# A two-block sequence model on one core: where the latent attention's keys are made

## The chip, the cores and the metric

The kernel runs on one core of a Trainium2 chip. Its time is the device time of one execution in microseconds (us); the median of three runs before the change is 2564.14 us (2563.71 to 2564.52). One more execution was profiled; it took 2568.02 us.

The engines are named as the profile names them: PE is the matrix engine (PEld its weight loads), ACT, DVE and POOL are the scalar, vector and GpSimd engines, SP issues most of the DMAs. Each engine works through its own instructions in order and waits at semaphores.

## The reference

Two transformer-like blocks over 512 tokens of width 1024, all in float32. The first block has three parts: a gated delta rule, a multi-head latent attention, and a feed-forward part. Only the attention matters here; cut to that:

```python
ckv = rms_norm(c_kv, kv_norm_w)                              # 512 x 256
k_nope = (ckv @ w_uk).reshape(B, S, 8, 128)                  # a key per head
v = (ckv @ w_uv).reshape(B, S, 8, 128)
k = concatenate([k_nope, broadcast(k_rope, 8 heads)], -1)    # 128 + 64
q = rms_norm(q, q_norm_w); k = rms_norm(k, k_norm_w)         # over all 192
... the last 64 of q and k are rotated by position
sc = einsum('bqhd,bkhd->bhqk', q[:, s0:s1], k[:, :s1]) * 192 ** -0.5
p = softmax(where(chunk mask, sc, -inf))                     # blocks of 128 queries
out = einsum('bhqk,bkhd->bqhd', p, v)
```

So for each head the key needs a projection (`w_uk`), the sum of squares of its 192 entries for each token, the inverse root of that, and a product with it.

## The kernel before, in words

One program is written out five times, once for each engine and once as a plan of the weights (`Plan`, `Tensor` for PE, `Scalar` for ACT, `Vector` for DVE, `Gpsimd` for POOL). Each stage is a generator; `program` (L813) runs them, and a `yield` is a step. `weave(main, side, n, m)` takes m steps of `side` over n steps of `main`. All engines take the same steps, so the order on every engine is fixed when the kernel is built.

Large linear layers work on one unit of weights at a time, 128x8x128 or 512 KB. SP loads it into one of three slots of `wraw`; ACT copies it to `whi` (rounded), then DVE (odd units) or POOL (even units) subtracts to get `wlo`; PE then does 24 passes of 512 columns for a unit (8 blocks of the input, each three times: `hhi,whi`, `hlo,whi`, `hhi,wlo`). I call these 24 passes a **layer step**. The call `ahead(i)` puts the splitting of all units up to number i+2 at that place of ACT's, DVE's and POOL's order. The units of `w_uk` (128 KB, one for each head) aren't split: PE multiplies straight from `wraw`, and their slot is free only when PE has done so. They are units of the same list and take slots of the same three.

While the attention runs, its steps are woven with the side work `beside`: the projections z0, z1, gd, gm and ya (layer steps), `o_norms` (the norms of the delta rule's output, matmuls with a matrix of ones), `z_gate` (eight Silu on ACT), `gates` (eight Sigmoid) and `split_o`. The main part is `norms_then`: `mla_norms` (values, last query norms, the five rotations) and then `mla_heads`, in which two heads go side by side, four pairs in all.

One head (`mla_head`) takes these steps:

- the key's projection on PE into a PSUM bank (`uk`); ACT squares it into `SCR[e]`; DVE adds the part of the rotary key (`SCR[e]+KQ`)
- a matmul with ones sums over partitions (`un`); ACT takes Ln and Exp of it, the inverse root; DVE multiplies the bank by it into `KN[e]` and the rotary key into `KZ[e]`; only then the bank of `uk` is free
- for the four blocks of queries: scores on PE (`mla_scores`), maximum on DVE, Exp on ACT, scaling on DVE, transposes on PE (`ps<-cst,...`), a copy on ACT, the product with the values on PE.

There is one `KN` and one `KZ` for even heads and one for odd ones, so the key of head h+2 can be written only after head h's last scores. Five PSUM banks (ps3 to ps7) serve all of the attention and the norms; ps0 to ps2 serve the layer steps. `KZ[e]` has 128 rows of which 64 hold zeros (set by POOL with one MEMSET behind the recurrence), so that it meets only its half of `QR`.

Of the kernel before, what the change touches and what calls it, by code (L numbers as in the profile page):

```python
# [7 lines left out]
P = 128  # L8
# [277 lines left out]
def build(nc, D, out, known):  # L286
# [5 lines left out]
    with ctx:  # L292
# [163 lines left out]
        KZ = [A[:, 18 + j, :] for j in range(2)]  # L456
# [5 lines left out]
        GM = [A[:, i, :] for i in (38, 39, 40, 41, 29, 23, 21, 22)]  # L462
# [115 lines left out]
        ADA_SUM = [SCR[3], SCR[4]]  # L578

# [72 lines left out]
        class Stages:  # L652
# [157 lines left out]
            prep = recur = early_norms = mla_norms = mla_head = o_norms = z_gate = gates = split_o = ple = conv = idle  # L810
            sv_norms = spatial = att_pairs = gla = idle

        def program(f):  # L813
# [17 lines left out]
            weave(f.norms_then(), side, 56, 38)  # L831
# [51 lines left out]
        class Plan(Stages):  # L883
# [51 lines left out]
            def mla_head(self, h):  # L935
                W.add(("uk", h), False, 2, P, [(rows(D["mla_w_uk"][0], 0, 2, h * P, P), 0)], ("ma_mm", "uk", h))
                for _ in range(11):
                    yield


        class Tensor(Stages):
# [372 lines left out]

            def mla_head(self, h):
                e = h % 2
                v = self.raw(("uk", h))
                bk = PA.take("uk", h)
                pe.wait_ge(*PA.free("uk", h))
                for k in range(2):  # L1320
                    pe.wait_ge(*at("mq_ve", "ck", k))
                    t = mm(bk[:, :], v[:, k, :], CKV[k], k == 0, k == 1)
                t.then_inc(*inc("ma_mm", "uk", h))
                yield
                bk = PA.take("un", h)
                pe.wait_ge(*PA.free("un", h))
                pe.wait_ge(*at("ma_ve", "sq", h))
                mm(bk[:, :], ones, SCR[e], True, True).then_inc(*inc("ma_mm", "un", h))
                PA.put(("un", h), "ma_act", "ln", h)
                PA.put(("uk", h), "ma_ve", "kn", h)  # L1330
                yield
# [26 lines left out]
            def mla_scores(self, h, i):  # L1358
                e = h % 2
# [6 lines left out]
                mm(bk[:, 0:Lk], ON[h][:, s], KN[e][:, 0:Lk], True, False)  # L1366
                pe.wait_ge(*at("ma_ve", "kz", h))
                pe.wait_ge(*at("ro_po", "r", h // 2))
                mm(bk[:, 0:Lk], QR[h // 2][:, s], KZ[e][:, 0:Lk], False, False)
# [213 lines left out]
        class Scalar(Stages):  # L1583
# [224 lines left out]

            def mla_head(self, h):
                e = h % 2  # L1810
                self.ahead(W.index["uk", h])
                ac.wait_ge(*at("ma_mm", "uk", h))
                ac.wait_ge(*(at("ma_ve", "kz", h - 2) if h >= 2 else at("mq_ve", "ck", 1)))
                act(SCR[e], PA.of("uk", h)[:, :], ACT.Square).then_inc(*inc("ma_act", "sq", h))
                yield
                ac.wait_ge(*at("ma_mm", "un", h))
                act(SCR[e], PA.of("un", h)[:, :], ACT.Ln, bias=kcol(K_EPS), scale=1.0 / 192).then_inc(*inc("ma_act", "ln", h))
                ac.wait_ge(*at("ma_act", "ln", h))
                act(SCR[e], SCR[e], ACT.Exp, scale=-0.5).then_inc(*inc("ma_act", "ri", h))
                yield  # L1820
# [446 lines left out]
        class Vector(Stages):  # L2267
# [291 lines left out]

            def mla_head(self, h):  # L2560
                e = h % 2
                rs = slice(64 * e, 64 * e + 64)
                self.ahead(W.index["uk", h])
                ve.wait_ge(*at("ma_act", "sq", h))
                ve.wait_ge(*at("mq_ve", "kq"))
                tt(ve, SCR[e], SCR[e], KQ, ALU.add).then_inc(*inc("ma_ve", "sq", h))
                yield
                ve.wait_ge(*at("ma_act", "ri", h))
                if h >= 2:
                    ve.wait_ge(*at("ma_mm", "s", h - 2, 3))  # L2570
                stt(KN[e], PA.of("uk", h)[:, :], col("kn"), SCR[e], ALU.mult, ALU.mult).then_inc(*inc("ma_ve", "kn", h))
                ve.wait_ge(*at("ro_po", "z"))
                tt(ve, KZ[e][rs], KR[rs], SCR[e][rs], ALU.mult).then_inc(*inc("ma_ve", "kz", h))
                yield
# [49 lines left out]
            def ev_gm(self, m, bk):  # L2624
                ve.wait_ge(*at(*lin_done("gm", m)))
                ve.wait_ge(*at("ro_po", "r", 3))
                cp(ve, GM[m], bk[:, :]).then_inc(*inc("mix_ve", "gm", m))

# [322 lines left out]
        class Gpsimd(Stages):  # L2951
# [92 lines left out]
            def mla_norms(self):  # L3044
# [4 lines left out]
                for p in SG.ends("rec"):  # L3049
                    po.wait_ge(*p)  # L3050
                ms(po, A[:, 18:20, :], 0.0).then_inc(*inc("ro_po", "z"))
# [6 lines left out]
            def mla_head(self, h):  # L3058
                self.ahead(W.index["uk", h])
                for _ in range(11):  # L3060
                    yield
# [252 lines left out]
```

## Time and profile before

| | us |
|---|---|
| median of three runs | 2564.14 |
| the profiled execution | 2568.02 |
| its span, first to last instruction | 2566.2 |
| PE busy in the span | 2361.6 |
| norms, attention and side work (628 to 951 us of the span) | 323 |
| PE busy in these 323 us | 276.1 |
| granted TensorE clock, whole span | 0.954 |

The page gives busy time per engine, and the chain of work that ended last: PE has 74% of it. The attention's stage lies from about 628 us (the rotations start) to 951 us (the output projection starts). Pairs of heads start at about 671, 713, 788 and 863 us. Times in rows are us from the start of the span. In rows of the time line the columns are start, length, engine, line, operation, and in brackets the idle time of that engine just before, with what ended it. `ps<-scr,cst` of 128x512 is the sum over partitions (`un`), `ps<-arena,wraw` the projection (`uk`), `ps<-nab` ends a block of scores.

### The profile page before, as it was taken

Reading aid. Unit: us, or ns where it says so; the run is one execution under the profiler, and the core shown is the slowest. Engines: PE = TensorE matmul, PEld = TensorE weight load, DVE = VectorE, ACT = ScalarE, POOL = GpSimd, SP = SyncE. Lnnn points to the kernel's source line nnn. Section 1 sums busy time; section 2 is a strip of 40 time slices with the busy share of each in tenths; the row PEclk is TensorE's granted clock in tenths of the full one; section 3 lists DMA queues with packets and bytes.
Section 4 is the critical chain, followed back from the end, with each engine's and each line's share of the span. In section 5 each row is a group of like instructions: output and inputs, shape, how many; then the busy total and the mean of one; then the engine's idle time right before and its main releaser. Section 6 shows DMA issues by size and latency. Waiting matters only on the chain.

```text
span 2566.2 us, 27004 instructions
## 1 busy us (share of the span) xinstructions
PE 2361.6 (92%) x10928; PEld 1894.9 (74%) x10928; DVE 1085.4 (42%) x1580; ACT 924.4 (36%) x1350; POOL 701.7 (27%) x416
## 2 busy tenths in 40 slices
PE   8798989999798899899999888999999999999996
PEld 4577877985566677688888676787777777888875
DVE  2576655454433332433321499513444243322333
ACT  2544423223432432533322332334552433322334
POOL 1141144002011125322223232321232353432332
PEclk9898989999899899899999898999999999999998
DMA  8222223121122124333333422232211322333341
GB/s 261 74 66 70 70 58 99 50 82 33 37 62 68 43 82 119 103 102 95 95 96 96 123 82 66 82 92 82 82 58 58 114 83 82 107 91 99 99 123 50
DMA packets 347983, 220.66 MB, mean 86 GB/s; under 512 B 18393, under 2 KB 327244, under 8 KB 347860
## 3 DMA queue, kind: packets, MB, share of 16 engines
q1 hardware_dynamic: 338462, 202.31, 27.3%
q10 hardware_dynamic: 9398, 16.62, 1.9%
q8 instruction: 88, 1.44, 0.2%
q14 instruction: 35, 0.29, 0.0%
HBM read 210.49 MB, written 8.41 MB: 85 GB/s over the span
## 4 chain that ended last, share of the span: by engine, by line
PE 74%; DVE 11%; ACT 8%; POOL 2%; issue 2%; DMA 2%; ACTq 0%; SPq 0%; DVEq 0%; POOLq 0%
PE ps L342 73%; DVE arena L368 4%; ACT arena L357 3%; DVE arena L360 2%; ACT scr L357 1%; DVE scr L368 1%; PE ps L345 1%; ACT whi L357 1%; POOL arena L360 1%; DMA wraw<-in_w_in_dram 1%; POOL wlo L360 1%; ACT L353 1%; DVE scr L360 1%; DVE wlo L360 1%; DVE arena L365 1%
## 5 line engine op out<-in xcount | busy, mean ns | idle before, releaser
L360 POOL TENSOR_TENSOR wlo<-wraw,whi 128x1024 fp32r<-128x1024 f32 (+1 forms) x163 | 390.8, 2398 | 1229.4 <-ACT whi L357 1229.4
L342 PE MATMUL ps<-hhi,whi 128*128 128x512 f32 x1664 | 678.3, 408 | 50.6 <-POOL wlo L360 31.2
L342 PE MATMUL ps<-hlo,whi 128*128 128x512 f32 x1664 | 661.9, 398 | 0.0
L342 PE MATMUL ps<-hhi,wlo 128*128 128x512 f32 x1664 | 661.2, 397 | 0.0
L357 ACT ACTIVATE whi<-wraw 128x1024 fp32r<-128x1024 f32 (+1 forms) x328 | 340.7, 1040 | 347.8 <-PE ps L342 294.7
L342 PEld LDWEIGHTS ps<-hhi,whi 128*128 128x128 f32 x1664 | 322.1, 194 | 131.6 <-issue 44.5
L342 PE MATMUL ps<-arena 128*128 128x128 f32 (+4 forms) x2304 | 337.1, 302 | 40.0 <-ACT arena L357 17.5
L342 PEld LDWEIGHTS ps<-hlo,whi 128*128 128x128 f32 x1664 | 322.0, 194 | 68.5 <-issue 3.7
L342 PEld LDWEIGHTS ps<-hhi,wlo 128*128 128x128 f32 x1664 | 320.8, 193 | 70.0
L360 DVE TENSOR_TENSOR wlo<-wraw,whi 128x1024 fp32r<-128x1024 f32 (+2 forms) x165 | 213.3, 1292 | 372.6 <-ACT whi L357 372.4
L342 PEld LDWEIGHTS ps<-arena 128*128 128x128 f32 x2304 | 291.4, 198 | 70.0 <-ACT arena L357 22.0
L357 ACT ACTIVATE arena<-ps 128x512 f32<-128x512 f32 (+5 forms) x223 | 116.6, 541 | 333.5 <-PE ps L342 269.0
L342 PE MATMUL ps<-h,whi 128*128 128x512 f32 x512 | 159.9, 394 | 1.1 <-POOL wlo L360 1.1
L357 ACT ACTIVATE scr<-ps,colv 128x512 f32<-128x512 f32 x78 | 55.5, 713 | 243.9 <-PE ps L342 243.7
L368 DVE SCALAR_TENSOR_TENSOR scr<-ps,colv,scr 128x511 f32<-128x511 f32 (+2 forms) x116 | 86.7, 748 | 132.9 <-ACT scr L357 130.5
L368 DVE SCALAR_TENSOR_TENSOR arena<-arena,colv 128x512 f32<-128x512 f32 (+1 forms) x136 | 131.7, 973 | 12.2 <-ACT arena L357 8.6
L360 DVE TENSOR_TENSOR arena<-ps,arena 128x512 f32<-128x512 f32 (+1 forms) x88 | 55.6, 639 | 147.4 <-PE ps L342 145.2
L360 DVE TENSOR_TENSOR scr<-ps,scr 128x512 f32<-128x512 f32 x86 | 59.1, 689 | 138.9 <-PE ps L342 137.2
L342 PEld LDWEIGHTS ps<-h,whi 128*128 128x128 f32 x512 | 97.2, 190 | 22.8 <-issue 2.6
L360 POOL TENSOR_TENSOR arena<-arena,scr 128x512 f32<-128x512 f32 x57 | 76.9, 1353 | 135.1 <-ACT scr L357 96.5
L342 PE MATMUL ps<-ff,whi 128*128 128x512 f32 x352 | 108.2, 389 | 0.0
L371 DVE COPY arena<-ps 128x512 f32<-128x512 f32 (+3 forms) x60 | 38.4, 652 | 150.3 <-PE ps L342 138.5
(190 smaller groups left out, 2729.1 us busy)
## 6 DMA issues: line engine op xcount, KB each, us to landing
wraw<-in_w_in_dram SPq DMA_DIRECT2D x99, 512.0 KB, 3.9
wraw<-in_w_ff_dram SPq DMA_DIRECT2D x64, 512.0 KB, 4.0
wraw<-in_ffn_w_up_dram SPq DMA_DIRECT2D x44, 512.0 KB, 3.8
wraw<-in_w_ada_dram SPq DMA_DIRECT2D x32, 512.0 KB, 3.9
wraw<-in_w_gate_dram SPq DMA_DIRECT2D x32, 512.0 KB, 3.9
arena<-in_w_ada_dram SPq DMA_DIRECT2D x8, 1024.0 KB, 11.5
wraw<-in_ffn_w_down_dram SPq DMA_DIRECT2D x16, 512.0 KB, 4.1
wraw<-in_w_branch_dram SPq DMA_DIRECT2D x16, 512.0 KB, 3.5
```

The source lines that it names most:

```text
L342: return pe.e.matmul(o, l, r, start=start, stop=stop)
L345: return pe.e.transpose(o, i, CST[0:n, C_ID:C_ID + n])
L353: ac.e.preload_act_table_set("natural_log_exp_and_others")
L357: return ac.e.activation(o, i, f, bias=bias, scale=scale, **kw)
L360: return q.e.tensor_tensor(o, a, b, op)
L365: return q.e.tensor_scalar(o, a, s1, s2, op0, op1)
L368: return ve.e.scalar_tensor_tensor(out=o, in0=a, scalar=s, in1=b, op0=op0, op1=op1)
L371: return q.e.tensor_copy(o, i)
```

## The change

`mla_head` loses its first two steps. They become `mla_keys(g)`, which makes the keys of both heads of a pair in three steps. `mla_heads` takes these steps for the next pair beside the present one (behind the steps 1, 3 and 5 of the pair, counted from 0), `norms_then` those of the first pair beside the norms. With it:

- the keys get tiles of their own: `KNB(h)` is in blocks 16/17, 40/41, 16/17, 54/55 of the arena for the four pairs, `KZB(h)` takes 64 rows of block 18 or 19, half each for the two heads; the rotary scores use 64 rows of both operands, and POOL's MEMSET goes
- the bank of `uk` is read earlier: DVE first writes `KNB = bank * col("kn")` (`kr`), which frees the bank, and later multiplies `KNB` by the inverse root in place, one DVE instruction more for each head
- new waits: `KNB` of heads 4 and 5 waits for the last scores of 0 and 1, that of head 6 for the projection of head 7 (blocks 54 and 55 hold the latent), `GM` gets another order of blocks, and its last two wait for scores of heads 2 and 3
- a head now has 9 steps in place of 11; the weave is 47 to 38 in place of 56 to 38.

```diff
+        def KNB(h):
+            return A[:, (16, 40, 16, 54)[h // 2] + h % 2, :]
+        def KZB(h):
+            return A[64 * (h % 2):64 * (h % 2) + 64, 18 + h // 2 % 2, :]
...
             def mla_heads(self):
                 for h in range(0, 8, 2):
-                    yield from both(self.mla_head(h), self.mla_head(h + 1))
+                    keys = self.mla_keys(h + 2) if h < 6 else iter(())
+                    for n, _ in enumerate(both(self.mla_head(h), self.mla_head(h + 1))):
+                        if n in (1, 3, 5):
+                            next(keys, None)
+                        yield
 
             def norms_then(self):
-                yield from self.mla_norms()
+                keys = self.mla_keys(0)
+                for n, _ in enumerate(self.mla_norms()):
+                    if n in (4, 5, 6):
+                        next(keys, None)
+                    yield
...
-            weave(f.norms_then(), side, 56, 38)
+            weave(f.norms_then(), side, 47, 38)
...
+            def mla_keys(self, g):                       # Vector
+                for h in (g, g + 1):
+                    self.ahead(W.index["uk", h])
+                    ve.wait_ge(*at("ma_act", "sq", h))
...
+                    ts(ve, KNB(h), PA.of("uk", h)[:, :], col("kn"), None, ALU.mult).then_inc(*inc("ma_ve", "kr", h))
+                    ve.wait_ge(*at("mq_ve", "kq"))
+                    tt(ve, SCR[h % 2], SCR[h % 2], KQ, ALU.add).then_inc(*inc("ma_ve", "sq", h))
+                yield
+                yield
+                for h in (g, g + 1):
+                    rs = slice(64 * (h % 2), 64 * (h % 2) + 64)
+                    ve.wait_ge(*at("ma_act", "ri", h))
+                    ve.wait_ge(*at("ma_ve", "kr", h))
+                    tt(ve, KNB(h), KNB(h), SCR[h % 2], ALU.mult).then_inc(*inc("ma_ve", "kn", h))
...
+                    tt(ve, KZB(h), KR[rs], SCR[h % 2][rs], ALU.mult).then_inc(*inc("ma_ve", "kz", h))
```

How instructions move, at three places. First PE at the end of the first pair of heads, before the change. `ps7<-arena` and `ps4<-arena` are the products with the values, `arena,wraw` the two projections, `scr,cst` the two sums.

```order
L342 MATMUL ps7<-arena 128x128 x3
L342 MATMUL ps4<-arena 128x128 [waits s_ma_act]
L342 MATMUL ps4<-arena 128x128 x3
L342 MATMUL ps4<-arena,wraw 128x512 [waits s_ob,s_raw1]
L342 MATMUL ps4<-arena,wraw 128x512
L342 MATMUL ps5<-arena,wraw 128x512 [waits s_raw2]
L342 MATMUL ps5<-arena,wraw 128x512
L342 MATMUL ps6<-scr,cst 128x512 [waits s_ma_ve]
L342 MATMUL ps7<-scr,cst 128x512 [waits s_ma_ve]
L342 MATMUL ps2<-hhi,whi 128x512 [waits s_w_lo_ve,s_w_hi,s_mix_ve]
```

The same place after the change: the products with the values, then a layer step (24 passes, cut here), then the scores of the next pair.

```order
L342 MATMUL ps7<-arena 128x128 x3
L342 MATMUL ps4<-arena 128x128 [waits s_ma_act]
L342 MATMUL ps4<-arena 128x128 x3
L342 MATMUL ps2<-hhi,whi 128x512 [waits s_w_lo_ve,s_w_hi,s_mix_ve]
...
L342 MATMUL ps7<-arena 128x128 [waits s_ob]
L342 MATMUL ps7<-arena 128x128 [waits s_ro_po]
L342 MATMUL ps7<-nab 128x128
```

The four instructions of the projections and the two sums are gone from this place. The projections now stand here, in the middle of the pair before, right behind its second block of scores and right ahead of a layer step:

```order
L342 MATMUL ps3<-arena 128x256 [waits s_ma_act]
L342 MATMUL ps3<-arena 128x256
L342 MATMUL ps3<-nab 128x128
L342 MATMUL ps5<-arena,wraw 128x512 [waits s_ma_act,s_raw0]
L342 MATMUL ps5<-arena,wraw 128x512
L342 MATMUL ps6<-arena,wraw 128x512 [waits s_ma_act,s_raw2]
L342 MATMUL ps6<-arena,wraw 128x512
L342 MATMUL ps2<-hhi,whi 128x512 [waits s_w_lo_po,s_w_hi,s_mix_ve]
```

The last row is the start of the layer step; it waits for both halves of its weights, the second of which POOL makes.

ACT at the same place, before: the Exps of the first two blocks of both heads with the splits of two units around them (`whi<-wraw`).

```order
L357 ACTIVATE whi<-wraw 128x1024 [waits s_mm,s_raw2]
L357 ACTIVATE arena,small<-ps3,small 128x128 [waits s_ma_ve]
L357 ACTIVATE scr,small<-ps5,small 128x128 [waits s_ma_ve]
L357 ACTIVATE arena,small<-ps6,small 128x256 [waits s_ma_ve]
L357 ACTIVATE scr,small<-ps3,small 128x256 [waits s_ma_ve]
L357 ACTIVATE whi<-wraw 128x1024 [waits s_mm,s_raw0]
L357 ACTIVATE arena<-ps5 128x128 [waits s_ma_mm]
```

And after: no split is left ahead of the four Exps, and three stand behind them, around the two squares of the next pair's keys (`scr<-ps5`, `scr<-ps6`).

```order
L357 ACTIVATE arena,small<-ps3,small 128x128 [waits s_ma_ve]
L357 ACTIVATE scr,small<-ps5,small 128x128 [waits s_ma_ve]
L357 ACTIVATE arena,small<-ps6,small 128x256 [waits s_ma_ve]
L357 ACTIVATE scr,small<-ps3,small 128x256 [waits s_ma_ve]
L357 ACTIVATE whi<-wraw 128x1024 [waits s_mm,s_raw1]
L357 ACTIVATE scr<-ps5 128x512 [waits s_ma_mm]
L357 ACTIVATE whi<-wraw 128x1024 [waits s_mm,s_raw0]
L357 ACTIVATE scr<-ps6 128x512 [waits s_ma_mm]
L357 ACTIVATE whi<-wraw 128x1024 [waits s_mm,s_raw1]
L357 ACTIVATE arena<-ps3 128x128 [waits s_ma_mm]
```

The first of the three splits belongs to the layer step that PE reaches right behind the projections: it used to be made a layer step earlier.

ACT also gets two table loads more, 67 in place of 65 in the whole program: four Silus now stand between the Exps of the first pair's third and last blocks (they stood behind the last), with a load on either side.

## Rows read from the trace of the kernel before

**Rows 1.** The page: busy time, clock in 40 slices, us to a DMA's landing.
```profile
PE 2361.6 (92%) x10928; PEld 1894.9 (74%) x10928; DVE 1085.4 (42%) x1580; ACT 924.4 (36%) x1350; POOL 701.7 (27%) x416
...
PEclk9898989999899899899999898999999999999998
...
wraw<-in_w_in_dram SPq DMA_DIRECT2D x99, 512.0 KB, 3.9
```

**Rows 2.** Stretches: width, busy of five engines, granted clock, DMA share, GB/s.
```profile
628.00:665.00 37.00, 23.51 (x45) 9.80 (x43) 16.75 (x19) 17.68 (x28) 14.42 (x10) 0.75 0.17 46
665.00:713.00 48.00, 42.29 (x197) 34.27 (x195) 16.94 (x43) 16.08 (x37) 2.39 (x1) 0.91 0.05 15
713.00:799.00 86.00, 74.36 (x317) 55.10 (x317) 33.01 (x59) 28.20 (x51) 11.87 (x5) 0.95 0.26 65
...
875.00:951.00 76.00, 66.85 (x293) 52.41 (x292) 27.36 (x51) 33.31 (x59) 16.16 (x9) 0.89 0.23 67
```

**Rows 3.** PE's waits from 628 to 952 us: total, times, longest.
```profile
PE ps L342 <- DVE scr L360: 16.3, 4, 5.7
PE ps L342 <- ACT arena L357: 11.7, 8, 5.0
PE ps L342 <- DVE arena L368: 10.7, 3, 7.1
PE ps L345 <- ACT arena L357: 3.6, 2, 3.3
```

**Rows 4.** Time line where the third pair starts.
```profile
787.86 3.59 PE L342 MATMUL ps<-arena,wraw 128*128 128x512 f32 x8
...
790.40 0.69 DVE L360 TENSOR_TENSOR scr<-scr,arena 128x512 f32<-128x512 f32 x1 [0.53 <-ACT scr L357]
...
793.70 1.06 ACT L357 ACTIVATE whi<-wraw 128x1024 fp32r<-128x1024 f32 x1 [3.33 <-DMA wraw<-in_w_in_dram]
...
794.84 2.35 POOL L360 TENSOR_TENSOR wlo<-wraw,whi 128x1024 fp32r<-128x1024 f32 x1 [24.18 <-ACT whi L357]
...
795.28 2.46 DVE L360 TENSOR_TENSOR scr<-scr,arena 128x512 f32<-128x512 f32 x1 [4.18 <-ACT scr L357]
...
797.79 2.07 PE L342 MATMUL ps<-scr,cst 128*128 128x512 f32 x2 [5.47 <-DVE scr L360]
...
803.43 0.39 PE L342 MATMUL ps<-hhi,whi 128*128 128x512 f32 x1
```

**Rows 5.** Time line where the norms end and the first pair starts.
```profile
657.46 2.08 PE L342 MATMUL ps<-scr,cst 128*128 128x512 f32 x2 [7.14 <-DVE arena L368]
...
661.76 3.78 PE L342 MATMUL ps<-arena,cst 128*128 128x512 f32 x4 [2.22 <-DVE arena L368]
...
664.56 1.42 PE L342 MATMUL ps<-hhi,whi 128*128 128x512 f32 x1
```

**Rows 6.** Time line of the second pair, behind its second block of scores.
```profile
734.69 0.41 PE L342 MATMUL ps<-nab 128*128 128x128 f32 x1
...
736.26 1.05 ACT L357 ACTIVATE whi<-wraw 128x1024 fp32r<-128x1024 f32 x1
...
737.38 2.39 POOL L360 TENSOR_TENSOR wlo<-wraw,whi 128x1024 fp32r<-128x1024 f32 x1 [14.98 <-ACT whi L357]
```

**Rows 7.** Time line around the Silus (first pair) and the Sigmoids (fourth pair).
```profile
701.24 1.28 ACT L357 ACT_TABLE_LOAD   x1
...
702.53 2.19 ACT L357 ACTIVATE arena<-arena 128x512 f32<-128x512 f32 x4
...
705.14 1.65 PE L342 MATMUL ps<-arena 128*128 128x128 f32 x6 [5.00 <-ACT arena L357]
...
887.98 0.48 PE L345 MATMUL ps<-cst,scr 128*128 128x128 f32 x1 [3.33 <-ACT arena L357]
```

**Rows 8.** PE's groups by shape, 500 to 960 us: busy, mean ns.
```profile
L342 PE MATMUL ps<-scr,cst 128*128 128x512 f32 x28 | 18.9, 764 | 23.4 <-DVE scr L360 16.3 <-DVE arena L368 7.1
...
L342 PE MATMUL ps<-scr,cst 64*128 64x512 f32 x12 | 6.7, 641 | 0.0
```

More of the change, by code:

```diff
@@ L461, in build @@
         MIX = [A[:, 30 + i, :] for i in range(8)]
[L462 removed]
+        GM = [A[:, i, :] for i in (38, 39, 29, 23, 21, 22, 40, 41)]
         XR = [A[:, 42 + i, :] for i in range(8)]
@@ L933, in build @@
             early_norms = steps(8)
[L935 to L938, printed above, removed]
+            def mla_keys(self, g):
+                for h in (g, g + 1):
+                    W.add(("uk", h), False, 2, P, [(rows(D["mla_w_uk"][0], 0, 2, h * P, P), 0)], ("ma_mm", "uk", h))
+                yield
+                yield
+                yield
+            mla_head = steps(9)
         class Tensor(Stages):
@@ L1313, in mla_norms, with mla_keys @@
                 yield
-            def mla_head(self, h):
[L1316 to L1331, printed above, removed]
+            def mla_keys(self, g):
+                for h in (g, g + 1):
+                    v = self.raw(("uk", h))
+                    bk = PA.take("uk", h)
+                    pe.wait_ge(*PA.free("uk", h))
+                    for k in range(2):
+                        pe.wait_ge(*at("mq_ve", "ck", k))
+                        t = mm(bk[:, :], v[:, k, :], CKV[k], k == 0, k == 1)
+                    t.then_inc(*inc("ma_mm", "uk", h))
+                    PA.put(("uk", h), "ma_ve", "kr", h)
+                yield
+                for h in (g, g + 1):
+                    bk = PA.take("un", h)
+                    pe.wait_ge(*PA.free("un", h))
+                    pe.wait_ge(*at("ma_ve", "sq", h))
+                    mm(bk[:, :], ones, SCR[h % 2], True, True).then_inc(*inc("ma_mm", "un", h))
+                    PA.put(("un", h), "ma_act", "ln", h)
+                yield
+                yield
+            def mla_head(self, h):
                 obk = PA.take("mo", h)
@@ L1365, in mla_scores @@
                 pe.wait_ge(*at("mq_ve", "qn", h))
-                mm(bk[:, 0:Lk], ON[h][:, s], KN[e][:, 0:Lk], True, False)
+                mm(bk[:, 0:Lk], ON[h][:, s], KNB(h)[:, 0:Lk], True, False)
                 pe.wait_ge(*at("ma_ve", "kz", h))
                 pe.wait_ge(*at("ro_po", "r", h // 2))
-                mm(bk[:, 0:Lk], QR[h // 2][:, s], KZ[e][:, 0:Lk], False, False)
+                mm(bk[:, 0:Lk], QR[h // 2][rs, s], KZB(h)[:, 0:Lk], False, False)
                 pe.wait_ge(*at("st_po", "nab"))
@@ L1807, in mla_norms, with mla_keys @@
                     yield
-            def mla_head(self, h):
[L1810 to L1820, printed above, removed]
+            def mla_keys(self, g):
+                for h in (g, g + 1):
+                    e = h % 2
+                    self.ahead(W.index["uk", h])
+                    ac.wait_ge(*at("ma_mm", "uk", h))
+                    ac.wait_ge(*(at("ma_ve", "kz", h - 2) if h >= 2 else at("mq_ve", "ck", 1)))
+                    act(SCR[e], PA.of("uk", h)[:, :], ACT.Square).then_inc(*inc("ma_act", "sq", h))
+                yield
+                for h in (g, g + 1):
+                    e = h % 2
+                    ac.wait_ge(*at("ma_mm", "un", h))
+                    act(SCR[e], PA.of("un", h)[:, :], ACT.Ln, bias=kcol(K_EPS), scale=1.0 / 192).then_inc(*inc("ma_act", "ln", h))
+                    ac.wait_ge(*at("ma_act", "ln", h))
+                    act(SCR[e], SCR[e], ACT.Exp, scale=-0.5).then_inc(*inc("ma_act", "ri", h))
+                yield
+                yield
+            def mla_head(self, h):
                 self.mla_exp(h, 0)
@@ L3056, in mla_norms, with mla_keys @@
                 yield
[L3058 to L3061, printed above, removed]
+            def mla_keys(self, g):
+                for h in (g, g + 1):
+                    self.ahead(W.index["uk", h])
+                yield
+                yield
+                yield
+            mla_head = Plan.mla_head
             o_norms, z_gate, gates = Plan.o_norms, Plan.z_gate, Plan.gates
```

42 lines of the change are left out of this document (22 added, 20 removed).

## The prediction

> **What bounds the kernel now.** I read the page first: PE is busy 92% of the span, the other engines 42% or less, and the clock's row falls below full speed at many places [rows 1]. So time is lost where PE idles or runs at 1.2 GHz. Next the table by stretches shows where this change works: between 628 and 951 us PE is busy 276 of 323 us, and the granted clock is lowest in the stretches where pairs start and norms end, 0.75 and 0.89 [rows 2]. The list of PE's waits then says for what. 16.3 us in four waits are for DVE's `scr` (the sum `SCR+KQ` of the keys), 10.7 us in three for DVE's `arena L368` (the key written from its bank), 11.7 and 3.6 us for ACT [rows 3].
>
> The time line shows the first kind [rows 4]. PE makes both projections (3.59 us). ACT's second square stands behind a split that waits 3.33 us for a DMA, because two of three weight slots were held by `w_uk`; then DVE's sum takes 2.46 us, and PE has nothing queued in between that is allowed to run: idle 5.47 us. When it restarts at 797.79, a pass of 512 columns takes twice as long until 803.43 (0.39 us in the row there; the start-to-start distance falls from 0.43 to 0.23 us): 1.2 GHz after the idle time, 2.4 GHz from then on. These 5.6 us at half speed cost 2.8 us more.
>
> The second kind is at the norms' end [rows 5]: `un` of head 1 waits 7.14 us for a DVE instruction, not for its data but for the bank that head 0's projection holds until its key is written, and the next norm waits 2.22 us for head 1's in the same way. The remaining 1.3 us of the 10.7 are in the last pair.
>
> **The change part by part.** The profiled execution took 2568.02 us, and the terms are taken from it; the median of the runs shown is 3.9 us lower.
>
> *Key chains at three pair starts.* The projections and sums leave the place where PE has nothing else, and get two layer steps and a block of scores between them. Their own work (8 passes in 3.59 us, so 0.45 each [rows 4], and 4 passes, 1.8 us) stays on PE. What goes is the idle time: 16.3 + 1.3 = 17.6 us [rows 3]. What is late next there: the scores of the next pair wait for the bank of `mo`, which ACT frees beside the layer step that now stands in between, so I take 0.
>
> *The clock behind them.* Three times 2.8 us [rows 4] = 8.4 us. In the last pair more runs slow: the clock of 0.89 over 76 us [rows 2] is 8.4 us of full speed lost, some of it while PE idled and some behind the Sigmoids, which stay. I give the key chain about half of it, 4.4 us, which is 1.6 more than the 2.8 counted. Bounds: 0, if the clock falls for other small gaps, and 12.
>
> *Norms and first pair.* The bank stalls go, 7.14 + 2.22 = 9.4 us [rows 5]: the bank is now free after the square and one DVE instruction. What is left is the chain of the output norms: four groups of two, each with two squares, the sums, Ln and Exp twice and two DVE products. ACT alone needs six activations for a group, some 3.5 us (four in 2.19 us [rows 7], a little more from PSUM), and DVE's rotations wait for POOL between them (POOL is busy 14.4 us here [rows 2]). 19 PE matmuls of two passes, 0.9 us, have to pass in the same order. Adding up group by group from 629 us, I get the first layer step at 653 with everything at its short duration, and 658 with DVE's and POOL's longer ones and some of it at 1.2 GHz, against 664.56 [rows 5]. I take 6.5 us; bounds 2 and 10. POOL's MEMSET lies in idle time of POOL: 0.
>
> *A weight split that comes later.* `ahead` counts `w_uk` as units, so the layer step behind the projections gets its `whi` only after the four Exps. By the times of the second pair [rows 6]: scores end at 735.10, ACT is done with the last Exp and starts the split at 736.26, `whi` ends at 737.31, POOL's `wlo` at 739.77, 4.7 us after the scores. PE has the projections to do, 3.6 us. New wait 1.1 us, in the first and second pair; in the third DVE makes `wlo` in half the time and two transposes lie in between, so 0. -2.2 us. The next split waits for a slot that the projection frees; 3.9 us for the DMA [rows 1] and 1.06 for `whi` end about 7 us behind the scores, and PE needs what ACT has queued behind it (copies of transposes) at 9.4 us at the earliest, in the third pair. So it hides, with some 2 us to spare. If that cover goes, each us counts.
>
> *Silus and Sigmoids.* Four Silus after the first pair's last Exp cost PE 5.00 us [rows 7]. After the change they stand ahead of the last two Exps, with a load on both sides: 1.28 + 2.19 + 1.28 = 4.75 us of ACT, during which PE has both last blocks of scores and two products (an estimate of 4.5 us, 22 passes of up to 512 columns). By my count PE then waits 0.35, 1.15 and 0.85 us, 2.35 in all: +2.6 us. At the Sigmoids of the last pair PE now arrives with full speed and waits 4.7 where it waited 0.94 + 3.33 [rows 7]: -0.4. The 0.78 us wait for ACT ahead of the second pair's projections goes: +0.8.
>
> By the Trainium skill ("ScalarE: Activation LUTs", What ACT_TABLE_LOAD costs) each switch costs 2.66 us, load and drain. The trace does not agree: the next activation starts 1.29 us after the load's start [rows 7]. By the page the two extra loads would cost ACT 5.3 instead of 2.6 us, and the sum would be up to 2.8 us smaller.
>
> *More DVE work.* Eight more products of two SBUF tiles. Bounds 0.69 and 2.46 us each [rows 4], 5.5 to 20 us of an engine that is busy for a third of this stage; the nearest rows beside an idle POOL say 0.69. On PE's path only in the norms, where it is in the 658 above. The second rotary matmul has 64 rows instead of 128: shapes of 64 rows took 641 ns, full ones 764 at both clocks mixed [rows 8], so 0. The second sum (`un`) waits for the Exp of the block just scored, about as long as the other head's block takes; I take -1.0 for what is over, bounds 0 and -3.
>
> Sum: 17.6 + 8.4 + 1.6 + 6.5 - 2.2 + 2.6 - 0.4 + 0.8 - 1.0 = 33.9 us. 2568.0 - 33.9 = 2534.1 for a profiled execution, 2564.1 - 33.9 = 2530 for the median.
>
> **The rivals.**
>
> *ACT stuck behind weights.* ACT's order now has three splits in a row behind the Exps, each waiting for a slot and a DMA. If the landing is late, ACT's copies are late and PE stalls in the middle of each pair instead of at its end. For it: 3.33 us of exactly this wait in [rows 4], and only 2 us of cover. Against it: PE has two layer steps of 5.5 us (24 passes of 0.23) there in two of three pairs. Price: 3.9 us (one landing) three times and the 8.4 us of the clock: 20 us, so 2550.
>
> *DVE and POOL in each other's way in the norms.* The keys' new products fall among POOL's ten rotation instructions. The same sum took 0.69 us with POOL idle and 2.46 with POOL's `wlo` beside it [rows 4]. If each of the eight DVE instructions of keys and norms there is stretched by up to 1.8 us, the stage gains nothing: 2530 + 6.5, and the clock stays low in it, 3 more: 2540. The Trainium skill ("SBUF — State Buffer", SBUF: two separate sides) says that a DVE instruction with two SBUF inputs and a GpSimd instruction exclude each other for the whole instruction. By that rule the trace agrees in the 2.46, which is POOL's end at 797.19 and a usual 0.69 less overlap.
>
> *Slower than before.* The four products that end the keys (two of `KNB`, two of `KZB`) stand on DVE between the Exps of the last scores and their scaling, for which PE's transposes wait. If all four take 2.46 us, and the scaling stands behind them, that is 9.8 us in each of three pairs, and 2.8 us of clock behind each: 38 us, against the 34 gained, so 2568. It decides from about 11 us per pair. Against it: POOL works only 11.9 us in 86 there [rows 2], so most of these instructions meet an idle POOL.
>
> *It does nothing.* PE's waits move to other places of equal length because weights bound the stage. Against it: the DMA share is at most 0.26 in the stage [rows 2]. 2564.
>
> **How the numbers follow.** Forecast 0.70 (2530), ACT behind weights 0.12 (2550), DVE and POOL 0.10 (2540), slower 0.05 (2568), nothing 0.03 (2564). The forecast's own bounds: all good ends (norms 10, clock 12, no waits) give 34 + 3.5 + 2 + 3 = 42, 2522; the bad ends (norms 2, waits twice, half of the clock) 34 - 4.5 - 3 - 5 = 21, 2543. With ACT's case the range goes to 2552, and I set its low end at 2518 for gaps whose clock cost I count nowhere. A measurement of this kernel can't tell less than 0.2% (5.1 us) from no change: faster 0.92, same 0.03, slower 0.05.
>
> **What the profile after will show.** PE's waits for DVE `scr` and `arena L368` in the stage fall from 27 to under 5 us; a new wait of about 1 us for POOL `wlo` behind the projections in two pairs; the first layer step after the norms starts 4 to 8 us earlier behind the last one of the norms; the wait at the Silus is split and about half; the one at the Sigmoids stays above 4 us; the clock of the pair starts is near 1.0, that of the last pair still below. The stage shrinks from 323 to about 289 us, everything behind it keeps its length. I'm wrong if PE waits for ACT `arena` grow by more than 5 us, or if the gap goes and the clock stays.

## The result and the profile after

The changed kernel takes 2551.06 us (median of 4 runs, 2550.77 to 2552.32) against 2564.2 us of the kernel before (4 runs beside it, 2563.71 to 2564.52), a ratio of 0.9947 with a 95% interval of 0.9935 to 0.9959. It is faster by 13.1 us where 33.9 were forecast: inside the range of 2518 to 2552, but at its slow end. Its profiled execution has a span of 2548.8 us, against 2566.2.

The stage by stretches, each from a pair start to the next one (columns as in [rows 2]):

```profile
628.00:664.00 36.00, 26.56 (x62) 12.41 (x61) 20.76 (x23) 18.71 (x30) 14.25 (x10) 0.86 0.08 22
664.00:720.00 56.00, 49.45 (x210) 34.38 (x209) 25.71 (x54) 24.61 (x47) 4.74 (x2) 0.94 0.16 43
720.00:791.00 71.00, 69.44 (x309) 50.87 (x307) 25.71 (x53) 22.74 (x42) 12.44 (x5) 1.00 0.27 71
791.00:855.00 64.00, 62.94 (x280) 45.80 (x280) 24.66 (x51) 23.76 (x45) 10.10 (x4) 1.00 0.27 75
855.00:932.00 77.00, 70.25 (x294) 51.54 (x293) 26.66 (x50) 28.78 (x53) 16.27 (x9) 0.91 0.21 61
628.00:932.00 304.00, 278.64 (x1147) 195.00 (x1146) 123.50 (x230) 118.59 (x217) 57.80 (x30) 0.95 0.21 58
```

And the stage of before as one row:

```profile
628.00:951.00 323.00, 276.10 (x1152) 204.52 (x1151) 118.78 (x222) 115.77 (x213) 54.37 (x29) 0.90 0.20 55
```

PE's idle time falls from 323.0 - 276.1 = 46.9 us to 304.0 - 278.6 = 25.4. The clock rises from 0.90 to 0.95, with two pairs at 1.00. Both came as forecast. But PE's *busy* time, which should shrink when the clock rises, grew by 2.5 us. PE is doing something longer.

PE's waits in the stage of after (628 to 945 us; total, times, longest):

```profile
PE ps L342 <- ACT arena L357: 10.7, 9, 4.9
PE ps L345 <- DVE arena L364: 4.6, 2, 3.8
PE ps L345 <- ACT arena L357: 4.0, 1, 4.0
PE ps L342 <- POOL wlo L360: 2.5, 2, 1.3
PE ps L342 <- DVE scr L360: 1.0, 1, 1.0
```

Against [rows 3] the 16.3 us for DVE's `scr` are 1.0 and the 10.7 us for DVE's key are gone. What PE does longer is seen in its own time line where the first pair starts. Before:

```profile
671.50 0.60 PE L342 MATMUL ps<-arena 128*128 128x128 f32 x4
671.86 0.30 PE L342 MATMUL ps<-nab 128*128 128x128 f32 x1
672.00 0.66 PE L342 MATMUL ps<-arena 128*128 128x128 f32 x4
...
672.56 1.08 PE L342 MATMUL ps<-arena 128*128 128x256 f32 x4
```

After:

```profile
664.10 0.80 PE L342 MATMUL ps<-arena 128*128 128x128 f32 x4
664.82 0.33 PE L342 MATMUL ps<-nab 128*128 128x128 f32 x1
664.99 0.85 PE L342 MATMUL ps<-arena 128*128 128x128 f32 x4
665.77 0.33 PE L342 MATMUL ps<-nab 128*128 128x128 f32 x1
665.93 1.27 PE L342 MATMUL ps<-arena 128*128 128x256 f32 x4
```

The first score block (four passes for nope and rotary, one for the mask) took 672.00 - 671.50 = 0.50 us and now takes 664.99 - 664.10 = 0.89. Nobody is waited for and the clock is full. The two blocks of 128 columns together: 1.06 before, 1.83 after. The weight loads' rows (660 to 930 us; busy and mean ns, then idle time before them) say where in the block it lies. After:

```profile
L342 PEld LDWEIGHTS ps<-arena 64*128 64x128 f32 x64 | 9.8, 192 | 15.1 <-issue 14.1
L342 PEld LDWEIGHTS ps<-nab 128*128 128x128 f32 x32 | 6.2, 192 | 15.1 <-issue 14.1
```

Before, the mask's row:

```profile
L342 PEld LDWEIGHTS ps<-nab 128*128 128x128 f32 x32 | 6.8, 213 | 3.5 <-issue 2.2
```

In after, 14.1 us of unexplained idle time ("issue") stand ahead of the 64-row loads and 14.1 ahead of the mask's 128-row loads that follow them. They are not the loss itself, since a load runs beside a matmul where nothing holds it, but they sit at exactly the two places of each block where the number of rows changes.

### The profile page after: what moved, and what is told of

Same layout as the page of the kernel before. It is cut to its first block, busy times and chain, and to the rows that moved or that the text cites. A ratio compares the mean times of both kernels' runs of the same rounds, so it can differ in the third digit from the quotient of the medians.

```text
span 2548.8 us, 27018 instructions
## 1 busy us (share of the span) xinstructions
PE 2361.8 (93%) x10928; PEld 1883.4 (74%) x10928; DVE 1090.6 (43%) x1588; ACT 926.9 (36%) x1352; POOL 699.7 (27%) x415
## 3 DMA queue, kind: packets, MB, share of 16 engines
q1 hardware_dynamic: 338462, 202.31, 27.3%
## 4 chain that ended last, share of the span: by engine, by line
PE 76%; DVE 11%; ACT 7%; issue 3%; POOL 2%; DMA 1%; ACTq 0%; SPq 0%; DVEq 0%; POOLq 0%
PE ps L342 74%; DVE arena L368 4%; ACT arena L357 3%; DVE arena L360 2%; DVE scr L368 1%; PE ps L345 1%; POOL wlo L360 1%; ACT whi L357 1%; ACT scr L357 1%; ACT L353 1%; POOL arena L360 1%; DVE wlo L360 1%; DVE arena L365 1%; DVE scr L360 0%; POOL scr L360 0%
## 5 line engine op out<-in xcount | busy, mean ns | idle before, releaser
L342 PEld LDWEIGHTS ps<-hhi,whi 128*128 128x128 f32 x1664 | 322.0, 194 | 134.7 <-issue 47.6
L342 PE MATMUL ps<-arena 128*128 128x128 f32 (+6 forms) x2304 | 341.6, 301 | 34.7 <-ACT arena L357 12.9
L342 PEld LDWEIGHTS ps<-arena 128*128 128x128 f32 (+1 forms) x2304 | 286.7, 197 | 70.0 <-issue 28.3
L368 DVE SCALAR_TENSOR_TENSOR arena<-arena,colv 128x512 f32<-128x512 f32 (+1 forms) x136 | 132.0, 975 | 16.3 <-ACT arena L357 12.6
L360 POOL TENSOR_TENSOR arena<-arena,cst 128x512 f32<-128x512 f32 (+1 forms) x48 | 62.2, 1309 | 144.3 <-PE ps L342 76.7
```

Source lines behind the costliest of these rows:

```text
L342: return pe.e.matmul(o, l, r, start=start, stop=stop)
L360: return q.e.tensor_tensor(o, a, b, op)
L368: return ve.e.scalar_tensor_tensor(out=o, in0=a, scalar=s, in1=b, op0=op0, op1=op1)
```

## The experiments

Theory T1: each change between 128 rows and 64 rows on PE costs time, twice in each of 32 score blocks. Rival T2: the shortfall went into waits and clock, and the longer blocks cover time in which PE would have waited anyway.

The medians carry some 3 us of noise. The programs are the same up to the stage, yet a mark in the norms (the restart behind the 1 us wait for `scr`) stands at 634.1 to 640.9 us in the executions profiled. So the length of the stage from that mark to the output projection is given beside the median: 931.87 - 634.96 = 296.9 us for the changed kernel. It comes from one execution each, and the same stage of the kernel before came out 3.0 us apart in two executions (below), so a difference of some 3 us in it is not told from noise either.

**The rotary matmul with all rows again** (the changed kernel otherwise):

```
-            return A[64 * (h % 2):64 * (h % 2) + 64, 18 + h // 2 % 2, :]
+            return A[:, 18 + h % 2, :]
-                mm(bk[:, 0:Lk], QR[h // 2][rs, s], KZB(h)[:, 0:Lk], False, False)
+                mm(bk[:, 0:Lk], QR[h // 2][:, s], KZB(h)[:, 0:Lk], False, False)
...
-                    if h >= 4:
-                        ve.wait_ge(*at("ma_mm", "s", h - 4, 3))
-                    tt(ve, KZB(h), KR[rs], SCR[h % 2][rs], ALU.mult).then_inc(*inc("ma_ve", "kz", h))
+                    ve.wait_ge(*at("ro_po", "z"))
+                    if h >= 2:
+                        ve.wait_ge(*at("ma_mm", "s", h - 2, 3))
+                    tt(ve, KZB(h)[rs], KR[rs], SCR[h % 2][rs], ALU.mult).then_inc(*inc("ma_ve", "kz", h))
...
+                ms(po, A[:, 18:20, :], 0.0).then_inc(*inc("ro_po", "z"))
```

> The changed kernel with one part of the change undone: the rotary score matmul gets all 128 rows again (KZ in two zero-padded tiles, one per head, written once the head before the last has been scored; one MEMSET on POOL more). Theory T1, the switch of the array from 128 rows to 64 and back costs about 0.4 us in each of 32 score blocks (0.50 became 0.89 us in the first block of 128 columns, 2.22 became 2.72 us in the one of 512): 12.9 us come back, 2551.1 becomes 2538, and PE's weight loads for the mask lose their idle time before them (15.1 us falls to about 3.5). Rival T2, the missing 20 us went into new waits for DVE, POOL and ACT and into the clock, and the longer blocks only show where PE would have waited anyway: within 2 us of 2551, PE's idle time in the stage grows by what the blocks lose.

Measured: 2535.95 us (2533.81 to 2537.67), ratio 0.9886, 0.9872 to 0.9901. 15.1 us came back; stage 917.36 - 634.61 = 282.8 us, 14.2 less. Its first pair and its mask loads:

```profile
663.71 0.60 PE L342 MATMUL ps<-arena 128*128 128x128 f32 x4
664.07 0.30 PE L342 MATMUL ps<-nab 128*128 128x128 f32 x1
664.22 0.66 PE L342 MATMUL ps<-arena 128*128 128x128 f32 x4
...
664.77 1.08 PE L342 MATMUL ps<-arena 128*128 128x256 f32 x4
```

```profile
L342 PEld LDWEIGHTS ps<-nab 128*128 128x128 f32 x32 | 6.2, 195 | 3.3 <-issue 2.2
```

The block takes 0.51 us again. The weight loads show what the change of rows does. In after, the first block of 256 columns (PEld):

```profile
665.87 0.30 PEld L342 LDWEIGHTS ps<-arena 128*128 128x128 f32 x2
666.51 0.29 PEld L342 LDWEIGHTS ps<-arena 64*128 64x128 f32 x2 [0.33 <-issue]
```

The same block with full rows:

```profile
664.71 0.73 PEld L342 LDWEIGHTS ps<-arena 128*128 128x128 f32 x4
```

With full rows the four loads follow each other, beside the matmuls. In after, the first 64-row load starts at 666.51, together with its own matmul, and not beside the pass ahead of it. The rows above merge instructions; the single records of the 512-column blocks give the price of one change. Passes of equal rows start 0.43 us apart, the first 64-row pass 0.52 behind the last 128-row one (698.38 - 697.86), and the second 64-row pass 0.53 behind the first: 0.09 + 0.10 = 0.2 us. The way back to 128 rows costs 0.2 us in the same way.

T2 is out: PE's idle time in the stage is 289.0 - 261.7 = 27.3 us, 1.9 more than in the changed kernel, while the busy time is 16.9 less.

```profile
628.00:917.00 289.00, 261.73 (x1145) 195.22 (x1143) 122.06 (x230) 118.13 (x216) 57.51 (x29) 0.96 0.22 61
```

**The kernel before with 64 rows, and nothing else:**

```
+                rs = slice(64 * e, 64 * e + 64)
-                mm(bk[:, 0:Lk], QR[h // 2][:, s], KZ[e][:, 0:Lk], False, False)
+                mm(bk[:, 0:Lk], QR[h // 2][rs, s], KZ[e][rs, 0:Lk], False, False)
```

> The kernel before with this one part of the change alone: the second score matmul reads only the 64 rows of its head (QR and KZ sliced), nothing else. T1: 32 blocks x 0.4 us, 2564.1 becomes about 2577. T2: no change, within 2 us of 2564; my prediction's step said 0 as well.

Measured: 2577.66 us (2576.87 to 2579.79), ratio 1.0048, 1.0032 to 1.0065: 13.3 us slower. The same two loads (660 to 950 us; busy and mean ns, then idle time):

```profile
L342 PEld LDWEIGHTS ps<-arena 64*128 64x128 f32 x64 | 10.6, 208 | 15.9 <-issue 15.0 <-DVE arena L360 0.2
L342 PEld LDWEIGHTS ps<-nab 128*128 128x128 f32 x32 | 6.6, 205 | 16.0 <-issue 15.2
```

So it is this part of the change alone, in both surroundings.

**The two 64-row matmuls side by side** (the changed kernel, other order in a block):

```
...
+                if h % 2:
+                    mm(bk[:, 0:Lk], QR[h // 2][rs, s], KZB(h)[:, 0:Lk], True, False)
+                    mm(bk[:, 0:Lk], ON[h][:, s], KNB(h)[:, 0:Lk], False, False)
+                    mm(bk[:, s], NAB[:, 0:P], NAB[:, P:2 * P], False, True)
+                else:
+                    mm(bk[:, 0:Lk], ON[h][:, s], KNB(h)[:, 0:Lk], True, False)
+                    mm(bk[:, s], NAB[:, 0:P], NAB[:, P:2 * P], False, False)
+                    mm(bk[:, 0:Lk], QR[h // 2][rs, s], KZB(h)[:, 0:Lk], False, True)
...
```

> The changed kernel (64-row rotary matmul) with another order of the three matmuls of a score block: the even head takes nope, mask, rotary, the odd head rotary, nope, mask, so that the two 64-row matmuls of a pair stand side by side and the array goes from 128 rows to 64 and back 16 times instead of 32. If the cost belongs to each switch from 128 rows to 64 and back (0.4 us), half of it returns: 2551 becomes about 2544.5, and PE's weight loads for the mask that stand behind a 128-row matmul lose their idle time. If it belongs to each 64-row matmul by itself, wherever it stands, 2551 stays. If the pair of 64-row matmuls even runs side by side in the array, it is below 2543.

Measured: 2545.14 us (2543.67 to 2546.83), ratio 0.9920, 0.9905 to 0.9935; stage 928.32 - 636.33 = 292.0 us, 4.9 less. The expected number came out, but my count of half the switches was wrong: in the blocks of 384 and 512 columns the product of the probabilities stands between the two heads' blocks, so only the first two sizes are joined, 8 places. There it is worth more than I said:

```profile
665.45 0.38 PE L342 MATMUL ps<-arena 128*128 128x128 f32 x2
665.59 0.30 PE L342 MATMUL ps<-nab 128*128 128x128 f32 x1
665.82 0.91 PE L342 MATMUL ps<-arena 64*128 64x128 f32 x6
666.49 0.30 PE L342 MATMUL ps<-nab 128*128 128x128 f32 x1
666.63 0.65 PE L342 MATMUL ps<-arena 128*128 128x256 f32 x2
...
668.59 0.65 PE L342 MATMUL ps<-arena,wraw 128*128 128x512 f32 x1
```

Two blocks of 128 columns take 666.63 - 665.45 = 1.18 us (1.83 apart, 1.06 with full rows), two of 256 take 1.96 (2.73 apart, 1.95 with full rows). Over four pairs of each that is 4 x 0.65 + 4 x 0.77 = 5.7 us, close to the 5.9 us of the medians. The mask's loads lost their idle time as expected, 15.1 us to 3.5.

One change there and one back for two blocks would leave 0.39 us above full rows, and only 0.12 and 0.01 are left. The rest is hidden because the two heads' 64-row matmuls, which use different halves of the rows, run beside each other: by the single records the four 64-row passes of 128 columns start at 665.82, 665.83, 666.04 and 666.04, and the next 128-row pass follows 0.42 us behind the first of them, where in after two such passes alone take 0.42 (664.41 to 664.82). With 256 columns four passes take 0.73 us, and two alone 0.63. So the cost does not belong to a 64-row matmul as such; it belongs to the change.

The cost of a block doesn't grow with its columns: for the pair of 512-column blocks with the product between them, 696.88 to 702.26 = 5.38 us in after and 694.20 to 698.80 = 4.60 with full rows, so 0.39 each, as in the blocks of 128 columns ((1.83 - 1.06) / 2). 32 x 0.39 = 12.5 us, 0.2 us per switch.

**Keys at each pair's own start** (full rows, the new tiles, the bank freed by one DVE instruction; nothing of the next pair beside the present one):

```
-                    keys = self.mla_keys(h + 2) if h < 6 else iter(())
-                    for n, _ in enumerate(both(self.mla_head(h), self.mla_head(h + 1))):
-                        if n in (1, 3, 5):
-                            next(keys, None)
-                        yield
+                    yield from self.mla_keys(h)
+                    yield from both(self.mla_head(h), self.mla_head(h + 1))
...
-            weave(f.norms_then(), side, 47, 38)
+            weave(f.norms_then(), side, 59, 38)
```

> The changed kernel with full rows as above, but each pair's keys are made at the pair's own start again, in the new tiles and with the bank that is freed by one DVE instruction; nothing stands between projection, sums and scores. If the gain comes from PE having other work during the key chain, the 17.6 us of idle time and some 8 us of clock come back as waits, and only the bank stall of the norms (9.4 us) may stay gone: 2555 to 2565. Rival: it was the early freed bank and the tiles that gained, then it is near the full-row kernel, about 2540.

Measured: 2562.17 us (10 runs, 2557.69 to 2567.28), ratio 0.9992, 0.9981 to 1.0004: no change to before that is clear of noise, 26.2 us above the same kernel with the keys beside, and inside the 2555 to 2565 that were expected. Its waits for the keys' sums:

```profile
PE ps L342 <- DVE scr L360: 19.4, 8, 4.8
```

So the move is what gains. The bank that is freed earlier has an effect of its own, but waits elsewhere take it back. From the last value projection on PE to the first layer step behind the norms it takes 656.10 - 610.77 = 45.3 us, against 53.6 and 52.2 in the two executions of before. In the pairs, on the other hand, PE waits 3.7 us for the keys' last products (1.36 before), and at the last pair 6.73 + 0.58 us where it was 3.33: DVE's scaling stands there behind three `hlo` products of 4.69 us in all.

**The kernel before once more:**

> The kernel before, unchanged, for a second profiled execution: the first one took 2568.0 us where the median is 2564.1. If the 3.9 us are of that one execution, this one is at 2564 and the output stage or another stretch is shorter in it; if profiling costs them, it is at 2568 again.

Measured: 2565.61 us, span 2563.8, so neither of my two values, 2564 and 2568. From the first wait for ACT in the norms to the output projection it takes 948.86 - 639.30 = 309.6 us, where the first execution took 951.03 - 638.48 = 312.6: the 3.0 us less are in the stage, with a clock of 0.92 instead of 0.90:

```profile
628.00:949.00 321.00, 272.69 (x1157) 202.74 (x1156) 119.48 (x224) 116.02 (x214) 54.56 (x29) 0.92 0.20 55
```

So 3.0 of the 3.9 us can have been that one execution. One more execution can't say what the rest is.

**Three ways to mend what the profile of after still shows**, all on the full-row kernel. The Silu wait, in the changed kernel (DVE and PE, 703 to 710 us):

```profile
703.26 2.60 DVE L360 TENSOR_TENSOR arena<-arena,scr 128x512 f32<-128x512 f32 x4
705.89 2.74 DVE L368 SCALAR_TENSOR_TENSOR arena<-arena,colv 128x512 f32<-128x512 f32 x4
...
708.74 0.49 DVE L364 TENSOR_SCALAR arena<-arena,small 128x512 f32<-128x512 f32 x1
...
709.28 1.12 PE L345 MATMUL ps<-cst,arena 128*128 128x128 f32 x4 [3.75 <-DVE arena L364]
```

The scaling for which PE waits stands on DVE behind four key products and four gating products.

```
             def z_gate(self):            # DVE
                 for g in (0, 4):
                     yield
+                    yield
                     for m in range(g, g + 4): ...
-                    yield
```

> The full-row kernel (2536) with DVE's first four gating products of the Silu step moved behind the scaling of the first pair's last block. In it these four take 2.7 us ahead of the scaling for which PE's transposes wait 3.75 us. If they are what remains of the Silu wait, the 3.75 falls to about 1.1 and the time by 2.6 us, to 2533.5. If the Silus themselves or the four key products hold the scaling up, less than 1 us.

Measured: 2535.58 us (2530.65 to 2539.44), by the median nothing, where 2.6 us were expected. But the profiled execution is the one whose mark stands at 640.85, and the slowest of its four; its stage is 919.72 - 640.85 = 278.9 us, 3.9 less, and the wait is as expected:

```profile
709.00 1.12 PE L345 MATMUL ps<-cst,arena 128*128 128x128 f32 x4 [1.11 <-DVE arena L364]
```

The split further ahead (in all three engines that split, `reach(i)` in place of `i + 3`; the condition is shortened):

```
+            def reach(self, i):
+                l = W.list
+                return min(i + (4 if ... l[i + 1] and l[i + 2] are "uk" units else 3), len(l))
```

> The full-row kernel with one weight split more made ahead where the next two units are the keys' weights, so that it stands on ACT and POOL in front of the four Exps of the last blocks of scores. PE's wait for POOL's wlo behind the projections, 1.28 and 1.34 us, goes: 2536 becomes 2533.4. If the split's DMA is not there yet, ACT waits for it in front of the Exps and the time goes up by some us.

Measured: 2534.98 us (2533.71 to 2536.52), 1.0 less by medians whose ranges overlap; stage 914.02 - 634.05 = 280.0, 2.8 less. Neither is clear of noise. What is shown is that both waits for `wlo`, 1.28 and 1.34 us, are gone.

Both of them:

> Both of the above on the full-row kernel: the two gains add up, 2536 becomes 2531. If they only move PE's wait to the next late thing, it stays near the better of the two alone.

Measured: 2528.28 us (2526.2 to 2528.53), ratio 0.9852, 0.9837 to 0.9867; stage 911.60 - 636.07 = 275.5, 7.2 less than with full rows alone. The two stage lengths add up to it (3.9 + 2.8). The medians do not: 0.4 and 1.0 us alone, 7.7 together. Together the gain is clear of noise; how it divides is shown by the waits alone.

**The norms and the gates**, on that kernel:

```
-                    if n in (4, 5, 6):
+                    if n in (4, 5, 8):        # norms_then: the first pair's products later
```

> The best version so far (2528.3: full rows, scaling first, split ahead) with the first pair's four key products moved behind the output norms' rotations on DVE. In it they stand as 5.32 us for four (0.69 each beside an idle POOL) ahead of the two products that ACT's squares wait for, and PE waits 4.92 us. If that order causes the wait, it falls to about 1 and the time by 4 us, to 2524.5. Rival, the norm stage is bound by POOL's rotations and ACT's chain anyway: the wait only moves to the next group, less than 1 us.

Measured: 2523.29 us (2521.2 to 2529.04), 5.0 less by the median, though the ranges overlap; stage 909.46 - 636.97 = 272.5, 3.0 less, in the slowest execution of the four. The waits of the norms behind the mark were 4.92 + 0.77 + 0.81 + 1.96 = 8.5 us and are now 1.57 + 0.49 + 1.10 + 0.48 + 3.73 = 7.4. The 4.92 went, but most of it turned up at the last group, as the rival said; the gain is nonetheless more than the rival's 1 us, and PE's busy time in the stage is 2.0 us less (252.2 against 254.2).

```
 def gates(self):    # ACT: all eight Sigmoids in the first of its two steps
 def z_gate(self):   # ACT: all eight Silus in the later step; DVE: their products one step behind
```

> The best version so far with the eight Silus in one step (the later of the two, beside a layer step) and the eight Sigmoids in one step (the earlier), so that neither stands between the Exps of two score blocks. PE's 4.43 us at the last pair go but for some 0.7 more ahead of the Exps of the first block, and of 0.77, 0.52 and 1.10 us at the first pair about 2 go: 5.5 us, 2528.3 becomes 2523. The rival, ACT and DVE lack the time behind (ACT's copies 2.2 us later, eight products of 5.5 us in a row on DVE): within 2 us of 2528.

Measured: 2521.44 us (5 runs, 2520.31 to 2525.64); stage 905.78 - 635.19 = 270.6, 4.9 less. The waits at the last pair's Sigmoids, 0.91 + 4.43, are now 1.50 + 0.34 + 0.75. At the first pair's Silus the expected 2 us did not come: 0.77 + 0.52 + 1.10 = 2.39 became 1.50 + 1.11 = 2.61. PE's idle time in the stage is 2.1 us less and its busy time 2.8 less, with the clock at 0.98 instead of 0.97 and 63 table loads in the program instead of 67.

Both of them:

> Both of the above: 2528.3 - 4 - 5.5 = 2519. Clock: each removed gap of over 4 us should also take a stretch at 1.2 GHz behind it away, up to 2.8 us each, so down to 2514.

Measured: 2520.36 us (2519.96 to 2520.94), ratio 0.9831, 0.9818 to 0.9845: 43.8 us below before, 30.7 below the changed kernel, and the lowest median here, though only 1.1 below the one before it. The 2519 was nearly met; the 2514 with the clock's extra gain was not. Stage 903.10 - 635.42 = 267.7 us; clock 0.99:

```profile
628.00:900.00 272.00, 254.97 (x1145) 191.54 (x1145) 119.03 (x227) 111.80 (x209) 57.16 (x29) 0.99 0.23 63
```

## Why the prediction was wrong

**The step that failed** is one sentence: "The second rotary matmul has 64 rows instead of 128: shapes of 64 rows took 641 ns, full ones 764 at both clocks mixed [rows 8], so 0." It cost 12.5 us by the rows, 13.3 us alone on before, 15.1 us when taken out of the changed kernel. The rows were read for the wrong thing, in two ways. First, the 764 ns are a mean over both clocks and the 641 ns are of full clock. At full clock the 64-row matmul is the longer one, as the rows of after show (660 to 930 us; busy, mean ns):

```profile
L342 PE MATMUL ps<-arena 64*128 64x512 f32 x16 | 9.0, 641 | 0.0
...
L342 PE MATMUL ps<-arena 128*128 128x512 f32 x16 | 8.2, 594 | 0.0
```

Second, what costs is the change to other rows, and the mean of a modelled duration doesn't show the distance from one start to the next. That distance stood in the trace of before too, where sums over 128 and over 64 rows follow each other in turn, at a clock of 1.00:

```profile
594.39 7.03 PE L342 MATMUL ps<-wraw,arena 128*128 128x512 f32 x16
601.26 4.18 PE L342 MATMUL ps<-arena,cst 128*128 128x512 f32 x8
605.37 0.50 PE L342 MATMUL ps<-hhi,whi 128*128 128x512 f32 x1
```

The sixteen full passes take 6.87 us, 0.43 each. The eight, which are two of 128 rows, two of 64, two of 128 and two of 64, take 4.11 us, 0.51 each; the starts of the single records lie 0.52 and 0.53 us apart at each change, so 0.2 us for one. Two changes in each of 32 blocks are 12.6 us, and the forecast could have had them. No bound above 0 was kept either, so neither a rival nor the range's arithmetic knew of it.

The Trainium skill ("TensorEngine Tiling (Array Packing)", Tiling Modes, Key Properties) says that a change of the tiling mode, not of the tile alone, makes the engine drain. If 64-row matmuls among 128-row ones count as such a change, which is my reading, the trace agrees: 0.2 us at each change of rows, the same with 128 and with 512 columns, and none to be seen between two 64-row matmuls on different halves.

The other steps, by their own terms:

- *Key chains, -17.6 us of idle time*: held. 16.3 us of waiting for `scr` became 1.0. Without the move, in the other tiles, it is 19.4. The 0.78 us wait for ACT ahead of the second pair's projections went as well.
- *The clock, -8.4 and -1.6*: held. The two middle pairs run at 1.00, where they ran at 0.95 and 0.98. The last pair went only from 0.89 to 0.91; with full rows it is 0.95. Clock below full speed times width, summed over the pairs, comes to some 21 us before and 10 after (an estimate, part of it falls where PE idled), and 10.0 were to be saved.
- *Norms, -6.5*: held. The first layer step starts at 657.5 instead of 664.56, of which 1.1 us are an earlier start of the whole stretch: counted from the last value projection (609.84 and 610.97) it is 5.9 us. The bank stalls of 7.14 and 2.22 went, and a wait for ACT of 4.92 came, which I had not named.
- *The later split, +2.2*: held: 1.27 and 1.28 us for POOL's `wlo` in the first two pairs, none in the third.
- *Silus, -2.6*: failed; the saving was put 2.9 us too large. Three waits of 0.26, 1.22 and 3.75 us, 5.2 in all, where I had 2.35. I counted ACT alone. The third is DVE's: its gating products wait for the Silus and stand, with the keys' products, ahead of the scaling.
- *Sigmoids, +0.4 slower*: 4.01 us instead of 4.7.
- *The second sum, +1.0*: did not come.

The sum with these steps at their size (the 64 rows, the Silus, the Sigmoids, the second sum): 33.9 - 12.5 - 2.9 + 0.7 + 1.0 = 20.2 us. From the last value projection to the output projection the time on PE fell from 951.03 - 610.97 = 340.1 us to 931.87 - 609.84 = 322.0, by 18.0; the last 2 us are not traced to a step. The profiled spans differ by 17.4, since behind the stage the execution of after is 1.8 us longer; its output projection begins at 1.2 GHz (two passes 1.09 us, 0.70 in before), a chance of the single execution: with other kernels of this study it took either value. The medians differ by only 13.1, mostly because the profiled execution of before was 3.9 us above its median. That is a flaw of the forecast of its own: waits counted in a slow execution were taken off the median.

With full rows the same stretch takes 307.9 us, 32.2 less than in the execution that the terms were taken from and 29.2 less than in the second one; by the medians the saving is 2564.4 - 2535.95 = 28.5 us. So the other steps together come near the 33.9.

Of the rivals none was what happened. The four key products of 2.46 us each did not occur: all four take 2.60 us in each of the three pairs. In the first pair they do stand ahead of the scaling, together with the gating products, and are part of the 3.75 us. ACT behind weights did not occur either. DVE and POOL in each other's way is real in the norms, where the four products take 5.32 us; moved behind the rotations they take 3.67, and the kernel gains 3 to 5 us, but that move also changed the order, so no run gives the price of the overlap alone. The time of 2550 that I gave to the rival of late weights was met, by another cause.

## What to carry to other kernels

Halving the rows of one matmul in a chain of full-height ones saved no time on PE here and cost 0.4 us for the way there and back. Pad to the full height with zeros, or gather the half-height matmuls next to each other. To price a change of shape, read the distance from start to start across the change, not the mean length of the group. And when a step is moved beside other work, look through every engine's queue for what now stands ahead of the thing that PE waits for.

## What the runs showed of the hardware

- Per score block of a 128-row, a 64-row and a 128-row matmul at full clock: 0.39 us more than with full rows, the same for 128, 256 and 512 columns, 0.2 us for each change. The pass at the change starts 0.09 us later than else and the one behind it 0.10 (after and before).
- Two heads' 64-row matmuls on different halves, side by side: four passes of 128 columns in 0.42 us, as long as two alone, and four of 256 in 0.73 us (the kernel with the two 64-row matmuls side by side).
- Half-height weights are not loaded quicker: 192 ns for each of the 64-row loads and for the mask's 128-row ones.
- The stage's clock is 0.90 where PE idles 46.9 of 323 us with waits of up to 7.14 us [rows 3], and 0.99 where it idles 17.0 of 272 us with waits of up to 3.73 (the last row of the experiments). No run tells the length of the waits from their sum.
- Four DVE products of two SBUF tiles took 2.60 us in the pairs and 5.32 among POOL's rotations in the norms (after).
